# The first mixer's projections as three fp32r products with the weights split in two

## The reference

```python
u = rms_norm(h, w_norm_mix)
proj = einsum('btd,dk->btk', u, w_in)          # conf_a, conf_g, z, xbc, dt_raw, gates
c = silu(layer_norm(depthwise_conv(conf_a * sigmoid(conf_g))))
branch_conf = einsum('btc,cd->btd', c, w_conf_out)
xbc = silu(depthwise_conv(xbc))                # then a scan in both directions gives y
y = rms_norm(y * silu(z), w_ssm_norm)
branch_ssm = einsum('btc,cd->btd', y, w_ssm_out)
merged = gates[..., :D] * branch_conf + gates[..., D:] * branch_ssm
h = h + einsum('btd,de->bte', merged, w_out)
```

## Time and profile before

| | us |
|---|---|
| median of three runs | 2524.82 (2522.86 to 2526.81) |
| the profiled execution, its own time | 2524.76 |
| its span in the profile | 2522.7 |
| TensorE busy | 2373.0 |
| VectorE busy | 1142.7 |
| ScalarE busy | 674.9 |
| GpSimd busy | 22.5 |

### The profile page before, as it was taken

One profiled execution on the slowest core, in us unless ns is written; L12 is line 12 of the kernel. 1 busy time (PEld: TensorE's weight loads), 2 busy tenths in 40 slices (PEclk: granted clock), 3 DMA queues, 4 the chain that ended last, 5 costly groups with the idle time before them and its releaser, 6 DMA issues. The chain is left out here.

```text
span 2522.7 us, 34246 instructions
## 1 busy us (share of the span) xinstructions
PE 2373.0 (94%) x13937; PEld 1577.1 (63%) x13937; DVE 1142.7 (45%) x2374; ACT 674.9 (27%) x1213; POOL 22.5 (1%) x38
## 2 busy tenths in 40 slices
PE   8999999989999888888898879999999999999998
PEld 6786777874222222222222236889999999888887
DVE  5657973131111111111111116238887776788887
ACT  2125564020000000000000002324454444454444
POOL 1000000000000000000000000000000000000000
PEclk9999999989999999999989989899999999999999
DMA  5365556737999999999999991324775555777775
GB/s 172 107 217 172 177 171 203 242 140 300 405 428 428 428 428 427 428 427 428 428 428 428 428 369 35 133 84 140 222 228 175 179 174 178 249 241 243 242 242 162
DMA packets 205420, 677.03 MB, mean 268 GB/s; under 512 B 15072, under 2 KB 137200, under 8 KB 180336
## 3 DMA queue, kind: packets, MB, share of 16 engines
q1 hardware_dynamic: 205296, 675.30, 72.3%
HBM read 657.40 MB, written 17.83 MB: 268 GB/s over the span
## 5 line engine op out<-in xcount | busy, mean ns | idle before, releaser
L549 PE MATMUL ps<-u,ring 128*128 128x272 f32 x1248 | 298.7, 395 | 4.1 <-DVE ring L387 2.9
L984 PE MATMUL ps<-ring,tokens 128*34 128x512 f32 x1248 | 273.6, 593 | 16.6 <-DMA ring<-in_w_up 16.6
L549 PEld LDWEIGHTS ps<-u,ring 128*128 128x128 f32 x1248 | 233.1, 190 | 55.8 <-issue 8.7
L2019 PE MATMUL ps<-m_hi,row_hi 128*128 128x256 f32 x1024 | 256.4, 288 | 0.8 <-ACT peer_s L2085 0.8
L1162 DVE TENSOR_TENSOR first_room<-first_room,ps 98x512 f32<-98x512 f32 x32 | 21.8, 682 | 505.7 <-PE ps L984 505.7
L2019 PE MATMUL ps<-m_lo,row_hi 128*128 128x256 f32 x1024 | 250.7, 283 | 0.0
L984 PE MATMUL ps<-extra_early,tokens 128*34 128x512 f32 x752 | 197.4, 676 | 14.7 <-DMA extra_early<-in_w_gate 11.8
L984 PEld LDWEIGHTS ps<-ring,tokens 128*34 128x34 f32 x1248 | 72.2, 112 | 215.2 <-issue 185.5
L1001 PE MATMUL ps<-ring,first_room 128*34 128x512 f32 x768 | 179.6, 614 | 25.5 <-DVE first_room L1166 23.0
L2019 PEld LDWEIGHTS ps<-m_hi,row_hi 128*128 128x128 f32 x1024 | 195.7, 191 | 1.6 <-issue 1.0
L2019 PEld LDWEIGHTS ps<-m_lo,row_hi 128*128 128x128 f32 x1024 | 196.1, 191 | 0.0
(11 more groups left out here) (398 smaller groups left out, 3015.7 us busy)
## 6 DMA issues: line engine op xcount, KB each, us to landing
ring<-in_w_down SPq DMA_DIRECT2D x48, 2048.0 KB, 22.4
ring<-in_w_up SPq DMA_DIRECT2D x47, 2048.0 KB, 24.5
ring<-in_w_gate SPq DMA_DIRECT2D x31, 2048.0 KB, 24.7
extra_early<-in_w_gate SPq DMA_DIRECT2D x31, 2048.0 KB, 18.5
ring<-in_w_in SPq DMA_DIRECT2D x36, 1024.0 KB, 5.4
extra_early<-in_w_up SPq DMA_DIRECT2D x16, 2048.0 KB, 25.7
extra_early<-in_w_down SPq DMA_DIRECT2D x16, 2048.0 KB, 25.4
rows<-in_peer_u SPq DMA_DIRECT2D x64, 512.0 KB, 3.7
```

Of the source, the lines that this page charges most:

```text
L549: last = pe.matmul(bank[:, 0:T], wt[:, k, c:c + P], src[:, k, :], start=k == 0, stop=k == kt - 1)
L984: last = pe.matmul(s.ps[HALF * j:HALF * j + CAP, 2 * c + u % 2, :], s.tokens[:, 2 * (u // 2) + k, :], rows[k][:, 1024 * c + 512 * j:1024 * ...
L2019: pe.matmul(out, hi[:, P * k:P * k + P], m[:, k, :], start=k == 0 and m is s.m2_hi, stop=False)
```

## The change

Each product of a projection becomes three with fp32r operands: upper part of the weights times upper part of the tokens, upper times lower, and lower times upper, summed in the same bank. The upper part is a copy rounded to fp32r (ScalarE), the lower part what is left (a subtraction).

- Weights are split in parts of eight blocks (128x1024; ssm has two parts a tile, 105 parts in all with dt's of half size). ScalarE rounds part n + 2 ahead of the evacuation of part n's tile (`round_weights`), into two buffers `w_hi`. The lower part is written over the weights in their slot (`t1_lower` is the ring's memory as fp32r), and `w_hi` is what was the ring's fourth slot. VectorE computes parts 0 to 3, GpSimd computes the other 101 in order (`lower_part`). GpSimd clears `s.decay` ahead of the part of tile a 4.
- The tokens are split once each: u, conf, y and the merged sum, the upper by ScalarE, the lower by VectorE, block by block. The scaling of y by `ssm_norm` moves into its split.
- `proj` issues for a part 16 products with the upper weights (upper and lower tokens in turn), then eight with the lower weights; the first two tiles run in three passes over both. dt waits for both weight parts.
- The ring of the mixer has three slots instead of four. `s.u_hi` and `s.u_lo` lie over `s.h` and `s.u`, so h is read again from memory while ssm runs, ahead of out.
- Of the four expert units loaded among the ssm units two remain; the other two move behind ssm, and the load behind out 3 waits for out 5.

The diff's core:

```diff
-    def __init__(self, slots, arrived, first=0):
...
+    def __init__(self, slots, arrived, ring=RING):
+        self.slots, self.arrived, self.ring, self.first = slots, arrived, ring, 0
+        self.loads = [0] * ring
...
+MIXER_RING = 3
...
+    parts, parts_of = [], {}
+    for t, (kind, _, unit, c) in enumerate(tiles):
+        if unit is not None:
+            parts_of[t] = []
+            for k0 in range(0, IT if kind == "ssm" else KT, KT):
+                parts_of[t].append(len(parts))
+                parts.append((t, unit, k0, c, 64 if kind == "dt" else P))
+    on_dve = [n for n in range(len(parts)) if n < 4]
+    on_pool = [n for n in range(len(parts)) if n not in on_dve]
+    lower = {n: (w_lo_dve, i + 1) for i, n in enumerate(on_dve)}
+    lower.update({n: (w_lo, i + 1) for i, n in enumerate(on_pool)})
...
+    def lower_part(eng, n):
+        return eng.tensor_tensor(lower_view(n), weights_of(n), upper_part(n).bitcast(F32), ALU.subtract)
...
             pool.memset(s.cb[:, :, :], 0.0).then_inc(masks, 1)
-            pool.wait_ge(cb_out, GROUPS)
-            pool.memset(s.decay[:, :, :], 0.0).then_inc(clean, 1)
+            for n in on_pool:
+                if parts[n][0] == pos["a", 4]:
+                    pool.wait_ge(cb_out, GROUPS)
+                    pool.memset(s.decay[:, :, :], 0.0).then_inc(clean, 1)
+                pool.wait_ge(w_hi, n + 1)
+                lower_part(pool, n).then_inc(w_lo, 1)
...
-            before = {tiles[pos["ssm", m]][2]: m - 1 for m in range(1, 5)}
+            before = {tiles[pos["ssm", m]][2]: m + 1 for m in range(1, 3)}
...
-                if i == ada[-1] + RING:
+                if i == ada[-1] + w.ring:
...
-                    sp.wait_ge(y_mid, IT)
                     s.load_expert_unit(sp, 0, AHEAD + before[i])
+                if i == tiles[pos["ssm", 3]][2]:
+
+                    sp.wait_ge(tiled, pos["gate", 2 * KT - 1] + 1)
+                    sp.dma_start(s.h[:, :, :], hT).then_inc(h_again, 16)
...
             s.load_expert_unit(sp, 0, AHEAD - 1, 0)
-            sp.wait_ge(tiled, pos["out", 3] + 1)
+            for u in range(AHEAD, AHEAD + 2):
+                s.load_expert_unit(sp, 0, u)
+            sp.wait_ge(tiled, pos["out", 5] + 1)
             s.load_expert_unit(sp, 0, AHEAD + 4)
...
+            def dve_lower(n):
+                dve.wait_ge(w_hi, n + 1)
+                lower_part(dve, n).then_inc(w_lo_dve, 1)
+
+            def lower_y(m):
+                dve.wait_ge(y_hi, m + 1)
+                dve.scalar_tensor_tensor(s.y_lo[:, m, :], s.xbc[:, m, :], s.col("ssm_norm")[:, m:m + 1], s.y_hi[:, m, :].bitcast(F32),
+                                         ALU.mult, ALU.subtract).then_inc(y_lo, 1)
+
+            def lower_m(m):
+                dve.wait_ge(m_hi, m + 1)
+                dve.tensor_tensor(s.u_lo[:, m, :], s.u[:, m, :], s.m_hi[:, m, :].bitcast(F32), ALU.subtract)\
+                   .then_inc(m_lo, 1)
...
+            for k in range(KT):
+                dve.wait_ge(u_hi, k + 1)
+                dve.tensor_tensor(s.u_lo[:, k, :], s.u[:, k, :], s.u_hi[:, k, :].bitcast(F32), ALU.subtract)\
+                   .then_inc(u_lo, 1)
+            for n in on_dve[0:4]:
+                dve_lower(n)
...
+                if m >= 3:
+                    for i in range(3 * m - 9, min(3 * m - 6, 13)):
+                        lower_y(i)
+            for i in range(13, IT):
+                lower_y(i)
...
+                    for n in parts_of[t]:
+                        k0 = parts[n][2]
+                        pe.wait_ge(w_hi, n + 1)
+                        for k in range(KT):
+                            for src, sem in ((hi, hi_sem), (lo, lo_sem)):
+                                if m == 0:
+                                    pe.wait_ge(sem, k0 + k + 1)
+                                last = pe.matmul(bank[:, 0:T], upper_part(n)[:, k, :], src[:, k0 + k, :],
+                                                 start=src is hi and k0 + k == 0, stop=False)
+                        last.then_inc(hi_used, 1)
+                        pe.wait_ge(*lower[n])
+                        for k in range(KT):
+                            last = pe.matmul(bank[:, 0:T], lower_view(n)[:, k, :], hi[:, k0 + k, :],
+                                             start=False, stop=n == parts_of[t][-1] and k == KT - 1)
...
+            def round_weights(n):
+                act.wait_ge(*w.ready[parts[n][1]])
+                if n >= 2:
+                    act.wait_ge(hi_used, n - 1)
+                    act.wait_ge(*lower[n - 2])
+                act.activation(upper_part(n), weights_of(n), ACT.Copy).then_inc(w_hi, 1)
+
             def evacuate(t):
                 kind, m, _, _ = tiles[t]
+                for n in parts_of.get(t, ()):
+                    round_weights(n + 2)
                 act.wait_ge(tiled, t + 1)
...
-                    act.activation(s.xbc[:, m, :], s.xbc[:, m, :], ACT.Copy, scale=s.col("ssm_norm")[:, m:m + 1])\
-                       .then_inc(y_scaled, 1)
+                    act.activation(s.y_hi[:, m, :], s.xbc[:, m, :], ACT.Copy, scale=s.col("ssm_norm")[:, m:m + 1])\
+                       .then_inc(y_hi, 1)
...
+            for n in range(2):
+                round_weights(n)
+            for k in range(KT):
+                act.wait_ge(normed, k + 1)
+                act.activation(s.u_hi[:, k, :], s.u[:, k, :], ACT.Copy).then_inc(u_hi, 1)
...
+                        act.wait_ge(silus, k + 1)
+                        act.activation(s.conf_hi[:, k, :], s.conf[:, k, :], ACT.Copy).then_inc(c_hi, 1)
...
+                round_weights(parts_of[pos["conf", 2 + half]][0])
             squares(WEIGHED[15] + (15,))
+            round_weights(parts_of[pos["conf", 4]][0])
             act.wait_ge(y_sum, IT)
             act.wait_ge(scaled, KT)
             act.activation(s.std[:, :], ps[:, 7, 0:T], ACT.Sqrt, bias=s.eps[:, 0:1], scale=1.0 / INNER).then_inc(ystd, 1)
+            for m in range(5, KT):
+                round_weights(parts_of[pos["conf", m]][0])
+            for n in parts_of[pos["ssm", 0]]:
+                round_weights(n)
             for m in range(KT):
+                for n in parts_of[pos["ssm", m]]:
+                    round_weights(n + 2)
+                act.wait_ge(evac_d, KT + m + 1)
+                act.activation(s.m_hi[:, m, :], s.u[:, m, :], ACT.Copy).then_inc(m_hi, 1)
```

More of the change, by code:

```diff
@@ L96, in add @@
     def add(self, src, a, b):
-        slot = (len(self.units) + self.first) % RING
+        slot = (len(self.units) + self.first) % self.ring
         self.loads[slot] += 1
@@ L229, in mixer @@
     tiles, ada = plan_mixer(s)
+    w.first = (w.ring - len(w.units)) % w.ring
     pos = {(kind, m): t for t, (kind, m, _, _) in enumerate(tiles)}
@@ L233, in mixer @@
              "c", "ada", "ada_out", "ada_sent", "ada_t", "xd", "row", "hsq", "router", "relu", "exped", "weighted", "pair", "y_out", "zsilu",
-             "y_mid", "squared", "y_sum", "y_scaled", "conf", "centred", "centred2", "scaled", "silu", "gates", "ystd", "merged")
+             "y_mid", "squared", "y_sum", "conf", "centred", "centred2", "scaled", "silu", "gates", "ystd", "merged",
+             "w_hi", "w_lo", "w_lo_dve", "hi_used", "u_hi", "u_lo", "y_hi", "y_lo", "c_hi", "c_lo", "m_hi", "m_lo", "h_again")
     (init, masks, squared0, sum0, std0, normed, tiled, evac_a, evac_d, neg, exp, w_out, log_out, aexp,
@@ L237, in mixer @@
      c_ready, ada_done, ada_out, ada_sent, ada_t, xd_ready, row, hsq, router, relued, exped, weighted, pair_done, y_out, z_done,
-     y_mid, squared, y_sum, y_scaled, conf_done, centred, centred2, scaled, silus, gates_done, ystd, merged_step) = (
+     y_mid, squared, y_sum, conf_done, centred, centred2, scaled, silus, gates_done, ystd, merged_step,
+     w_hi, w_lo, w_lo_dve, hi_used, u_hi, u_lo, y_hi, y_lo, c_hi, c_lo, m_hi, m_lo, h_again) = (
         s.sem(f"mix_{k}") for k in names)
@@ L486, in _ @@
             store_ada(HALVES - 1)
+            for k in range(KT):
+                dve.wait_ge(c_hi, k + 1)
+                dve.tensor_tensor(s.conf_lo[:, k, :], s.conf[:, k, :], s.conf_hi[:, k, :].bitcast(F32), ALU.subtract)\
+                   .then_inc(c_lo, 1)
             for m in range(KT):
@@ L523, in proj @@
                 kind, m, unit, c = tiles[t]
-                if unit is not None:
-                    wt = w.wait(pe, unit)
                 if t >= 2:
@@ L637, in _ @@
             last.then_inc(sum0, 1)
-            wt = w.wait(pe, tiles[0][2])
-            for k in range(KT):
-                pe.wait_ge(normed, k + 1)
-                for t in range(2):
-                    last = pe.matmul(ps[:, t, 0:T], wt[:, k, P * t:P * t + P], s.u[:, k, :], start=k == 0, stop=k == KT - 1)
-                    if k == KT - 1:
-                        last.then_inc(tiled, 1)
+            pe.wait_ge(w_hi, 2)
+            for src, sem in ((s.u_hi, u_hi), (s.u_lo, u_lo)):
+                for k in range(KT):
```

(10 more changed lines are left out.)

73 lines of the change are left out of this document (53 added, 20 removed).

## The result

The changed kernel takes 2645.64 us (median of four runs, 2626.74 to 2647.83) against 2525.82 (2522.86 to 2526.97) for the kernel before: 1.046 times as long, 95% interval 1.041 to 1.0509. The forecast was 2578 us, its range 2520 to 2620. The direction was right; the loss is 120 us where 53 were forecast. The changed kernel's runs spread over 21 us, those of the kernel before over 4. The profiled execution has a span of 2641.5 us, 118.8 more than before.

What follows compares the result with a forecast made beforehand. TensorE was busy 94% of the span, VectorE nine tenths between roughly 200 and 360 us. Terms 27.4 + 40.9 - 3.5 + 3 - 10.4 - 4.7 = +52.7 us on 2524.82 gave 2578 us, range 2520 to 2620.

Steps and rivals of the forecast that it cites:

- The products: TensorE's projections: an fp32r product takes 0.1256 us, a part of eight falls from 3.67 to 3.01 us.
- The subtraction on GpSimd: GpSimd's lower parts of the weights: 1.94 us for each of 101 subtractions, with 1.06 as the lower end.
- two-pass reasoning: GpSimd's subtraction: both inputs come through one reader one after the other, 2048 numbers, so 1.94 us.
- L: VectorE time lost to each GpSimd subtraction wherever two-SBUF-input work waits: 1.94 + 0.14 = 2.08 us.
- the sum: First mixer, stage by stage with L = 2.08: gains and losses total +52.7 us.
- The base until pair 0: Before pair 0: VectorE's chain of groups takes 161.3 us without stalls; 32 L = 66.6 more gives 227.9.
- the rival without blocking: Whole kernel: long two-input instructions might share the reader; pair 0 near 180 us, total 2486 us; chance 0.12.
- The waits in the pairs: Pairs 0 to 12: blocked time uses up most of VectorE's 14.6 us of waits for exponentials; 4 us kept.
- The clock: Rival in the pairs: TensorE idles and a quarter of each pair runs at 1.2 GHz; +35, 2613 us; chance 0.08.
- The bytes are hidden: Until pair 0: loads through three slots cost nothing; in the a/g stage VectorE is behind by more than the lead.
- conf: Conf stage: eight tiles gain 5.2 us, ScalarE's added work costs 8 us, a loss of 3.
- The argument by VectorE's idle share: Ssm stage: VectorE is idle four fifths, so L costs nothing and the gain is 10.4 us.

Runs made afterwards that it cites:

- e8_ssm_out: Changed kernel with only ssm and out split into fp32r products, all projections before them left fp32, conf too; median 2512.7 us, 0.994 to 0.9967 of the kernel before.
- e1_memset: Changed kernel with every GpSimd subtraction replaced by three fills of the same tile that read nothing; median 2529.1 us, 1.0007 to 1.0028 of the kernel before.
- e5_memset_light: Changed kernel with fills in place of GpSimd's subtractions and ada units loading only their first block; median 2503.2 us, 0.99 to 0.9931 of the kernel before.
- e4_light_ada: Changed kernel with each ada unit loading only the first of its eight blocks, used eight times; median 2633.6 us, 1.0407 to 1.0452 of the kernel before.

## Why the forecast was right in direction and half the size

**The products.** 0.1256 us each, 6.03 us an ssm tile: measured as forecast (481.18 - 475.15, in e8_ssm_out). Out gives 0.67 us a tile. This part held wherever TensorE had its full clock, and it is all that the change has to give.

**The subtraction on GpSimd.** 2.50 us where I took 1.94. My two-pass reasoning gave the lower of the two prices that I had, and the Trainium skill's figure (GPSIMD Engine Reference, section 3.1, some 2.25 us for this size, an estimate) was nearer, but still below the trace.

**What a subtraction takes out of VectorE.** L was 2.08 us. In the pairs 27 cost 52.3 us, 1.94 each (194.9 against 142.6 us with memsets); the sum had 54.1. The mechanism held. That the size held too is partly luck: the subtraction is 0.56 us longer than I took it, and on average a fifth of that time cost VectorE nothing, which I had left out. The rule of the Trainium skill (SBUF — State Buffer, "Who interferes with whom") is borne out by e1_memset. The trace adds that one reading instruction of GpSimd can be kept waiting through dozens of VectorE's; the sum had no term for that.

Of the 66 us that the sum missed by, 25.0 lie ahead of pair 0, 28.4 in the pairs and 12.7 behind them.

**The base until pair 0: the first step that failed.** The sum said 161.3 us without stalls plus 66.6 of stalls. With memsets, so without GpSimd's reading, pair 0 starts at 196.4; the reading costs 56.5 on top. The base was 35 us too low, and the stalls 10 too high, which hid part of it. The numbers to see it were there: TensorE was busy 188.5 us until pair 0; take away 0.65 us for each of its parts, about 26, and add the 12 us that it was idle, and it alone needs some 174 (an estimate). I had chained VectorE's groups as if TensorE, ScalarE's roundings and the loads had delivered everything at once. Of the 22 us between 174 and 196, 5.9 are the loads (e5_memset_light); the rest stays open. The same error sits in the rival without blocking (pair 0 near 180, 2486 us): measured without GpSimd's reading it is 2529.

**The waits in the pairs: the second.** I let the blocked time use up most of VectorE's waits and kept 4 us. It used up none of them: the waits are 34.9 us with GpSimd's reading and 34.2 with memsets, and the 52.3 us of blocked time came wholly on top. Nor did they stay at their old 17.2 us. With memsets, light ada units take them to 19.9 us and the extra products on TensorE to 26.9 (171.0 - 144.1), so late loads and the clock both feed them; in the changed kernel light ada units leave them at 33.9 and the extra products take them to 15.9 (214.2 - 198.3), about what they were before. The clock was a rival of its own with chance 0.08 and a price of 35 us. It did fall, to 0.81, and its price is some 16 us. It should have been a term of the sum, since the sum itself made TensorE idle 5 us in each pair.

**The loads: the third.** "The bytes are hidden" was argued for the a/g stage by VectorE being behind anyway. With the stalls there the price is 6.5 to 12 us by e4_light_ada, ahead of pair 0; without them 19 to 26.

**conf: the fourth.** Forecast for everything behind pair 13: -15.6 us; measured -2.9, and -14.5 with memsets. Pairs 13 to 15 and conf together were to gain 0.5 us; they lose 8.3, and gain 0.3 with memsets. So ScalarE's queue was a loss of the size that I gave it, and what failed is that conf had no term for GpSimd's reading: y_lo and the evacuation behind it stand on the path. The argument by VectorE's idle share was made for ssm, where it holds: -8.8 us measured, -8.0 with memsets, -10.4 forecast.

Together, by profiled executions: 121.1 us hang on GpSimd's reading (56.5 + 53.0 + 11.6), and the change without it is at -2.3 us, its 14.5 us of late gain eaten by 12.2 us of rounding, loads and clock before pair 13. By the medians, the safer number, the first is 116.5 and the second +4.4. The parts don't add up exactly, since the clock and the starved subtractions (15.3 us ahead of pair 0 for the one that was moved) are also consequences of the stalls.

## What to carry to other kernels

Give an idle GpSimd work that reads SBUF only where VectorE has little to read there itself: beside a busy VectorE each such microsecond cost about 0.8 of VectorE's (52.3 us for 27 subtractions of 2.50), and doing it on the busy engine itself was cheaper here (1.22 us against 1.94). Before trusting a chain summed along one engine, hold it against what the other engines alone need in the same stretch. A faster product pays only where TensorE is the only one late: here in ssm and out, and there alone the change is worth 12 us.

## What the runs showed of the hardware

- The stall has no fixed loser: GpSimd's 2.5 us subtraction took 17.18 us behind 44 back-to-back taps of VectorE, while taps elsewhere waited 2.1 us for each subtraction of GpSimd. A copy of 1.05 us took 16.17 us at the same place. What decides which of them goes first was not settled.
- A memset on GpSimd leaves VectorE's two-input instructions as they are (489 against 493 ns) and slows its one-input tap from 414 ns, undisturbed, to 698. Readings slow both kinds: the two-input taps take 573 ns on average beside copies and 710 beside subtractions, and a one-input tap that starts at 49.86 us, beside a subtraction from 49.70 to 52.20, takes 2.50 us.
- VectorE's instructions with one input in PSUM keep their time beside the subtractions: gate_z's take 429 ns, 427 in the kernel before.
- Fifteen useless products a pair went with a kernel 16 us faster and a granted clock of 0.98 instead of 0.81 in the pairs; six a pair, with memsets on GpSimd, with 8.4 us and 0.97 instead of 0.92.
